# A ring of weight slots planned with other block times, and the second and third blocks' token rows fetched ahead of the routed experts' weights

## The reference

```python
for i in range(DEPTH):
    shift, scale, gate = adaln(cond, w_mod[i], b_mod[i])       # six vectors of 1024 per layer and condition
    x = x + g1 * mixer_i(modulate(x, norm_mix[i], sh1, sc1))
    x = x + g2 * moe(modulate(x, norm_ffn[i], sh2, sc2), ...)

def moe(h, ...):
    gates = top2_of_best_group(sigmoid(h @ w_router))          # (tokens, 16), two are not zero
    a, u = h @ w_gate[e], h @ w_up[e]                          # 1024 -> 256, for every expert e
    return sum_e((silu(a) * u * gates[:, e]) @ w_down[e])      # 256 -> 1024
```

## Time and profile before

| | |
|---|---|
| runs of the kernel before | 1649.26 us median of 3 (1647.81 to 1649.79) |
| profiled execution | 1657.81 us; span of its instructions 1656.0 us |
| TensorE busy | 1454.0 us, 88% of the span, granted clock 0.947 |
| VectorE, ScalarE, GpSimd busy | 556.2, 371.9 and 226.7 us |
| DMA | 417.21 MB, 252 GB/s over the span |

### The profile page before, as it was taken

One profiled execution on the slowest core, in us unless ns is written; L12 is line 12 of the kernel. 1 busy time (PEld: TensorE's weight loads), 2 busy tenths in 40 slices (PEclk: granted clock), 3 DMA queues, 4 the chain that ended last, 5 costly groups with the idle time before them and its releaser, 6 DMA issues.

```text
span 1656.0 us, 26585 instructions
## 1 busy us (share of the span) xinstructions
PE 1454.0 (88%) x10752; PEld 862.8 (52%) x10752; DVE 556.2 (34%) x1362; ACT 371.9 (22%) x985; POOL 226.7 (14%) x304
## 2 busy tenths in 40 slices
PE   3999998988997997997989999989869999969974
PEld 1876774323775774332564557743227766843221
DVE  1237343212456424211522442432105266242115
ACT  1106321110214521111211442211102045211110
POOL 0100122101121022111100001221011000221111
PEclk9999999998998998999899999999989999979997
DMA  9996148999788138899858403489997871247981
GB/s 328 320 320 196 77 173 292 384 413 349 262 304 233 78 134 280 305 421 349 296 197 246 120 1 153 173 298 387 399 345 258 280 270 55 98 164 302 422 338 56
DMA packets 122788, 417.21 MB, mean 252 GB/s; under 512 B 13659, under 2 KB 55614, under 8 KB 98086
## 3 DMA queue, kind: packets, MB, share of 16 engines
q1 hardware_dynamic: 95414, 345.08, 56.2%
q0 software_dynamic: 20304, 66.47, 12.2%
q10 hardware_dynamic: 6944, 3.91, 0.8%
HBM read 389.21 MB, written 28.76 MB: 252 GB/s over the span
## 4 chain that ended last, share of the span: by engine, by line
PE 70%; DVE 9%; DMA 8%; issue 6%; ACT 3%; POOL 1%; ACTq 1%; SPq 0%; another core or an unknown queue 0%; DVEq 0%; POOLq 0%
PE bank L1825 61%; DMA ring<-in_moe_w_gate 4%; PE bank L1995 3%; DMA hT<-h_rows,id_of 2%; PE bank L2159 2%; ACT pp L1147 2%; DMA ring<-in_moe_w_down 2%; ACTq L670 1%; PE bank L1882 1%; POOL small L804 1%; DVE xn L1294 1%; PE bank L2043 1%; DVE gbc L1291 1%; DVE xn L1304 1%; DVE hT L1281 0%
## 5 line engine op out<-in xcount | busy, mean ns | idle before, releaser
L1825 PE MATMUL bank<-ring,pp 128*32 128x512 f32 x2272 | 365.5, 634 | 40.6 <-DMA ring<-in_moe_w_down 27.9
L1825 PE MATMUL bank<-ring,hT 128*128 128x256 f32 (+3 forms) x998 | 234.9, 394 | 4.3 <-DVE kT L1590 2.6
L1825 PEld LDWEIGHTS bank<-ring,hT 128*128 128x128 f32 x998 | 182.5, 192 | 53.4 <-issue 27.9
L1825 PE MATMUL bank<-work,pp 128*32 128x512 f32 x816 | 183.9, 612 | 12.1 <-issue 9.2
L1825 PEld LDWEIGHTS bank<-ring,pp 128*32 128x32 f32 x2272 | 95.4, 116 | 167.1 <-issue 165.6
L1825 PE MATMUL bank<-ring,xn 128*128 128x256 f32 x768 | 168.2, 380 | 0.0
L1825 PEld LDWEIGHTS bank<-ring,xn 128*128 128x128 f32 x768 | 145.0, 190 | 19.4
L1825 PE MATMUL bank<-V,pp 128*32 128x512 f32 x512 | 131.0, 637 | 14.5 <-issue 11.6
L1715 DVE TENSOR_TENSOR pp<-bank,pp 128x256 f32<-128x256 f32 x40 | 17.0, 425 | 345.2 <-ACT pp L1224 345.2
L1147 ACT ACTIVATE pp<-bank,neg_max 128x384 f32<-128x384 f32 x192 | 96.6, 524 | 13.0 <-DVE neg_max L1606 10.1
L1825 PEld LDWEIGHTS bank<-work,pp 128*32 128x32 f32 x816 | 48.5, 112 | 94.5 <-issue 93.9
(11 more groups left out here) (275 smaller groups left out, 1800.1 us busy)
## 6 DMA issues: line engine op xcount, KB each, us to landing
ring<-in_w_mod SPq DMA_DIRECT2D x76, 1024.0 KB, 7.3
ring<-in_moe_w_gate SPq DMA_DIRECT2D x40, 1024.0 KB, 16.4
ring<-in_moe_w_up SPq DMA_DIRECT2D x40, 1024.0 KB
ring<-in_moe_w_down SPq DMA_DIRECT2D x37, 1024.0 KB, 14.5
work<-in_moe_w_down SPq DMA_DIRECT2D x16, 1024.0 KB, 7.9
y_slots<-kT POOLq DMA_DIRECT2D x32, 512.0 KB, 9.1
gbc<-in_w_mod SPq DMA_DIRECT2D x14, 1024.0 KB, 9.7
work<-in_moe_w_gate SPq DMA_DIRECT2D x12, 1024.0 KB
```

The source lines that it names most:

```text
L1825: return pe.matmul(out, lhsT, rhs, start=start, stop=stop)
```

## The change

The planner's block time goes from 11.8 to 12.05 us, the down tiles' first use from 11.0 to 18.3 us and their last from 18.5 to 22.8 us after their blocks' starts, and the stage starts 2 us later in the plan. d(12) to d(15) may now also stand in slots that only gate/up tiles used. mod(L+1,0,0) and mod(L+1,0,1) may use only slots 2 and 3, so that slots 0 and 1 can take an expert's pair early; the other six may use 4 to 7 and slot 13, which then waits for the mixer's last gate multiplication. DVE does `near_rows` ahead of `hold`, and `near_ids` ahead of its copy of block 0's rows. PE does `slot_ids` between the two halves of `gather_rows`. POOL issues two of the six writes to `ids`, then the rows of blocks 1 and 2, then tells SP (`near_issued`), then the other four writes. SP waits for both `held_ready` and `near_issued` before g(4).

```diff
@@ -193,13 +193,13 @@
         at = run_mods(mods["route"][:4], now + 52.0)
         run_mods(mods["route"][4:], at + 3.0)
         mark["held", L] = now + 68.0
-        now += 73.0
+        now += 75.0
         for e in range(E):
             for part in ("moe_g", "moe_u"):
-                begin[part, L, e], end[part, L, e] = now + 11.8 * first_block(e), now + 11.8 * last_block(e) + 7.5
-            begin["moe_d", L, e] = now + 11.8 * first_block(e) + 11.0
-            end["moe_d", L, e] = now + 11.8 * last_block(e) + 18.5
-        now += 11.8 * BLOCKS + 20.0
+                begin[part, L, e], end[part, L, e] = now + 12.05 * first_block(e), now + 12.05 * last_block(e) + 7.4
+            begin["moe_d", L, e] = now + 12.05 * first_block(e) + 18.3
+            end["moe_d", L, e] = now + 12.05 * last_block(e) + 22.8
+        now += 12.05 * BLOCKS + 19.0
         mark["summed", L] = now
     return begin, end, mark
 
@@ -219,10 +219,13 @@
         pairs = ((0, 1), (2, 3), (8, 9), (10, 11)) + (((4, 5),) if key[2] >= FIXED else ())
         return [pair if name == "moe_g" else pair[1:] for pair in pairs]
     if name == "moe_d":
-        return [(slot,) for slot in (6, 7, 12) + ((13,) if last_block(key[2]) < 7 else ())]
-    if name == "wo" or phase == "route" and key[2] == 1:
+        late = (13,) if last_block(key[2]) < 7 else tuple(range(6)) + (8, 9, 10, 11) if key[2] >= E - FIXED else ()
+        return [(slot,) for slot in (6, 7, 12) + late]
+    if name == "wo":
         return [(slot,) for slot in (4, 5, 6, 7)]
-    if name == "ukv" or phase == "route":
+    if phase == "route":
+        return [(2,), (3,)] if key[2:] in ((0, 0), (0, 1)) else [(slot,) for slot in (4, 5, 6, 7, 13)]
+    if name == "ukv":
         return [(slot,) for slot in (0, 1, 2, 3)]
     if name == "mod" and key[2] < 2:
         return [(slot,) for slot in range(R)]
@@ -237,6 +240,8 @@
         if slot in (10, 11):
             return mark["turned" if KINDS[L] < 2 else "heads", L]
         return mark[late[slot], L] if slot in late else 0.0
+    if part == "route":
+        return mark["mixed_in", L] if slot == 13 else 0.0
     return mark["summed", L - 1] if part == "main" and slot in (9, 13, 14) and L > 0 else 0.0
 
 
@@ -489,8 +494,8 @@
         rows_ready, wk_ready, over_ready, h_out, xT_full, xT_a, xT_v, ids_zeroed, ids_out, held_ready = (sem(s) for s in
             ("rows_ready", "wk_ready", "over_ready", "h_out", "xT_full", "xT_a", "xT_v",
              "ids_zeroed", "ids_out", "held_ready"))
-        near_ready, ids_full, ids_ready, ids_in, ov_t_in = (sem(s) for s in
-            ("near_ready", "ids_full", "ids_ready", "ids_in", "ov_t_in"))
+        near_ready, near_issued, ids_full, ids_ready, ids_in, ov_t_in = (sem(s) for s in
+            ("near_ready", "near_issued", "ids_full", "ids_ready", "ids_in", "ov_t_in"))
         g_in, y_out = [sem("g_in0"), sem("g_in1")], [sem("y_out0"), sem("y_out1")]
         (ov_idx_ready, ov_g_in, ov_xT_full, ov_xT_ready, ov_w_in, ov_au_full, ov_sil,
          ov_act, ov_acT_full, ov_acT_ready, ov_y_full, ov_y, ov_y_out) = (sem(s) for s in
@@ -706,10 +711,10 @@
                         sp.wait_ge(comb_used, 3 * L - 1)
                     elif slot == 14:
                         sp.wait_ge(x_moe_v, 3 * L)
+                elif slot == 13 and part != "main":
+                    sp.wait_ge(wo_mul, 12 * (L + 1))
                 elif part == "moe":
-                    if slot == 13:
-                        sp.wait_ge(wo_mul, 12 * (L + 1))
-                    elif slot in (10, 11) and KINDS[L] < 2:
+                    if slot in (10, 11) and KINDS[L] < 2:
                         wait_evacuated(sp, *[("qT", L, p) for p in range(8)], *[("kT", L, g) for g in range(G)])
                         sp.wait_ge(states, 32 * (L + 1))
                     elif slot >= R:
@@ -748,6 +753,7 @@
                     return
                 if (L, FIXED) not in held_at and e >= FIXED:
                     sp.wait_ge(held_ready, L + 1)
+                    sp.wait_ge(near_issued, L + 1)
                     held_at[L, FIXED] = None
                 if held_at.get((L, e)) is None:
                     at = e - FIXED
@@ -909,10 +915,13 @@
                 pool.wait_ge(rows_ready, L + 1)
                 if L == 0:
                     pool.wait_ge(ids_zeroed, 16)
-                for b in range(NB):
+
+                def ids_by_slot(b):
                     for k in range(2):
                         nc.gpsimd.indirect_dma_start(ids, rows_at(row_of[:, k, b:b + 1]), own_id[:, b:b + 1], None,
                                                      bounds_check=last_slot, oob_is_err=False).then_inc(ids_out, 16)
+
+                ids_by_slot(0)
                 pool.wait_ge(h_out, 48 * (L + 1))
                 pool.wait_ge(ids_ready, L + 1)
 
@@ -943,6 +952,9 @@
 
                 block_in(1)
                 block_in(2)
+                pool.sem_inc(near_issued, 1)
+                ids_by_slot(1)
+                ids_by_slot(2)
                 later_ids()
                 if L > 0:
                     pool.wait_ge(comb_full, 6 * L)
@@ -1688,8 +1700,8 @@
                 evacuate(*[("hrow", L, 2, half) for half in range(2)])
                 places(L)
                 slot_rows(L, picks)
+                near_rows(L)
                 hold(L)
-                near_rows(L)
                 pick_weights(L, picks)
                 overflow(L)
 
@@ -1707,8 +1719,8 @@
                     dve.wait_ge(ys_free, n + 1)
                     V_.tensor_copy(ys[:, blk % 2, 512:1024], bank[5][:, :]).then_inc(y_v, 1)
 
+                near_ids(L)
                 turned_rows(BLOCKS * L, 0)
-                near_ids(L)
                 for blk in range(BLOCKS):
                     n, slot = BLOCKS * L + blk, blk % 2
                     dve.wait_ge(sil_full, n + 1)
@@ -2232,6 +2244,8 @@
                     pe.wait_ge(xT_v, n + 1)
                     wait_evacuated(pe, *[("hrow", L, b, half) for b in range(NB) for half in range(2)])
                     for k in range(KC):
+                        if k == KC // 2:
+                            slot_ids()
                         for b in range(NB):
                             ins = mm(bank[6 + k // 4][:, k % 4 * P:(k % 4 + 1) * P], xn[:, b, k * P:(k + 1) * P],
                                      first_of[:, b, :], b == 0, b == NB - 1)
@@ -2284,7 +2298,6 @@
                     ins.then_inc(ids_full, 1)
 
                 gather_rows(BLOCKS * L)
-                slot_ids()
                 for blk in range(BLOCKS):
                     n, slot = BLOCKS * L + blk, blk % 2
                     block_gate_up(blk)
```

## The result

The changed kernel takes 1602.9 us (median of 4 runs, 1597.0 to 1608.5), the kernel before in the same comparison 1649.5 us: a ratio of 0.971, 95% interval 0.966 to 0.976. The prediction was 1601 us with a range of 1582 to 1630. A second comparison on the chip gave 0.973 (0.969 to 0.976). The profiled execution took 1606.3 us, with a span of 1604.5 us, 51.5 us less than before.

What follows compares the result with a forecast made beforehand. TensorE, busy 88% of the span, was taken as the bound, with late expert tiles setting the stage's end. Terms -51 + 1 + 1 = -49 us on 1657.8 gave 1609, in proportion 1601 us; range 1582 to 1630.

Steps and rivals of the forecast that it cites:

- The planner's list: Experts' stage: new tile order and slots let d(15) land earlier, gaining 10, 12, 18 and 11 us per layer, 51 us.
- The signs I named: Expected trace: no 15 us SP stand, d(15) issued over 10 us before last down, 405 GB/s over some 90 us.
- The anchor of the stream: Experts' stage: tile transfers counted from near_issued, with d(15) landing 127 us after it, 7 us of that for gaps.
- the slower rival: g(4) starts 8.6 us later per layer and the delay reaches the last down: 1669 us at 350 GB/s; chance 0.06.
- Near rows and numbers: Block 1's wait for gathered rows, 13.7 us in three layers, goes; none of it counted as gain, only as cover.
- The new wait: TensorE waits 2.6 to 3.9 us for the eighth modulation tile in layers 1 and 2; charged 1 us in all.
- The sum: All terms together: -51 + 1 + 1 = -49 us on the profiled 1657.8 us, in proportion 1601 us.
- slot_ids: Between the halves of block 0's rows: some 1.2 us, hidden in layers 0 to 2, about 1 us in layer 3.
- A gap that stays: Rival: pauses in the experts' tile stream remain or open elsewhere, giving 1636 us, or 1620 with half; chance 0.17.
- The late third gather: Rival: four later table writes delay block 3's rows, costing 5 us in three layers: 1616 us; chance 0.06.
- More: Rival: no gap and free table writes give 11 us more per layer, about 1577 us; chance 0.06.
- The ceiling of 358 GB/s: Rival: HBM loads can't pass 358 GB/s, so each layer ends about 2 us later: about 1659 us; chance 0.02.

Runs made afterwards that it cites:

- old modulation slots: The changed kernel with the eight modulation tiles back in the slots they had before the change: 1590.7 us, ratio 0.963; again 1601.0 us, 0.968.
- the front alone: Kernel before, old planner, with only near rows' numbers first, two gathers ahead of four table writes, and near_issued ahead of the first routed tile: 1653.3 us, 1.001.
- the modulation tile first: The changed kernel with the eighth modulation tile moved ahead of g(3), u(3) in SP's order, slots unchanged: 1594.2 us, ratio 0.966.
- both edits on the kernel before: Kernel before with the new block times and the new slots of the last four down tiles, modulation tiles and front as before: 1615.0 us, 0.976.
- the down slots alone: Kernel before with only the last four down tiles also allowed in slots that only gate/up tiles used: 1650.7 us, ratio 0.996.

## Why the prediction was right

The time was right to 2 us and the mechanism of the main term was right. That it came out so close is luck: the main term was too small by some 20 us, and the loss by the new wait too small by nearly as much.

- **The planner's list.** Predicted -51 us, by `near_issued` 10.8 us after the start of block 0's rows and d(15) landing 127 us behind it: 551 us over four layers from these rows to the last down. Measured 530.4, which is 72.2 less than before: g(4) leaves 7.1 to 9.0 us after the rows' start, and d(15) lands 123.1 to 124.9 us after g(4). Of the 72.2 us the stretch from block 2 to the last down has 59.5. The signs I named are all there: no 15 us stand of SP, d(15) out 20 us ahead of the last down, 414 GB/s for 80 us, short waits for tiles before block 7's down and block 9's gate/up (2.41 and 1.11 us). What I did not see is that it takes two edits. Block times order the gate/up pairs ahead of the downs, slots let the last downs go; one without the other moves the wait to the other end of the queue.
- **The anchor of the stream.** The step "d(15) lands 2.3 + 114 + 4 + 7 = 127 us after `near_issued`" has the right size for a wrong reason. The stream starts at the end of block 2's gate/up, which lies 31 to 32 us after g(4) in this kernel anyway. The run without the wait for `near_issued` tells the two apart: g(4) 7.1 us earlier, d(15) as late as before. The 8.6 us by which g(4) would be late, on which the slower rival rested, therefore cost nothing.
- **Near rows and numbers.** The step that failed is "I count none of it, since the down tiles set the end and these microseconds turn into waiting before block 9". The gather's wait went, as predicted, but it lies ahead of block 2 and so on the path. What that is worth depends on the rest. With the old modulation slots it is 12 us in the first column (169.0 to 156.9) and 14 us by medians. With the change's own slots it is 4 to 7 us by the ratios, inside the intervals, and 3.3 us in the first column (160.9 to 157.6): most of the 12.7 us there come with the planner. Alone it is worth nothing, as the run of the front alone shows. So for the change itself the step was wrong by little.
- **The new wait.** The charge of 1 us was mis-sized: the eighth modulation tile takes 6.30, 6.23 and 6.88 us of waiting, not 1.4 and 2.6 to 3.9. It lies on the path by the same anchor. In layer 0 the tile was issued at 249.0 behind g(3), u(3) and landed at 260.7, 11.6 us later, where I had 2.3 + 3 x 2.6 = 10.1. I had also counted it as covered by the gather's wait, which was itself no cover. After the wait the tile's records take 1.93 us where they take 1.07 without it. Moving the tile ahead brought 20.7 us back in the third column.
- **The sum.** -72.2 from the rows' start to the last down and +20.7 in all the rest (19.4 of it this wait), against my -51 and +2. The errors, 21.2 and 18.7 us, cancel to 2.5 us.
- **slot_ids.** 1.2 us predicted, 1.40 measured (266.33). It is not hidden in layer 0, where the rows' second half starts behind it.
- **The rivals.** A gap that stays: there is one, up to block 2 (282 GB/s), but from there none. The late third gather hardly came in the change (block 3's gather goes out at 291.2 in layer 0; its rows cost 0.2 and 0.6 us in layers 1 and 2). It came, with 7.6 to 9.7 us in all, in every run that has four table writes behind the gathers and no long wait for a modulation tile: the front alone, the modulation tile first, the old modulation slots. With the long wait it stays below 1 us a run. That the wait gives the table its time is my reading of this pattern; no run tests it. The rival "More" was priced wrong: by the prediction's own numbers TensorE is ready 128.1 us after the rows' start, which is 88 us of gain and some 1562 us, not 1577. The ceiling of 358 GB/s: the trace disagrees with that rule of the Trainium skill (page "DMA: Bandwidth & Descriptors", section "Where 436 GB/s comes from") less than I had put it. The 414 GB/s from 301 to 381 hold six stores of 0.52 MB, 39 GB/s, so loads alone ran at about 375 GB/s. That is still above the rule's figure, and the change gained.

What stays open: why the old modulation slots cost 10 to 15 us between block 2 and the last down (388.4 to 389.3 in the second column against 372.8 to 379.1). Late rows of block 3 are part of it where the front is new (8.5 and 7.9 us), but the run of both edits on the kernel before has none and shows 388.6. There TensorE's waits between the marks are 26.1 us against 15.4 in the change; they stand ahead of block 9's gate/up (2.8 to 4.3 us) and, in three layers, of the last down (3.2 to 4.5 us). Why the old slots make these tiles later I have not followed. Open too is whether these slots or the tile moved first are faster than the change by more than the spread of runs. No run has all three columns at their best; 154.6, 372.8 and 1053.4 would together make a span of some 1581 us, an estimate that takes the columns as independent.

## What to carry to other kernels

Before summing the work of a stream of transfers, find the tile that waits for a compute step and behind which the queue never runs empty. Here what delayed that step delayed the end, and the tiles that left ahead of it had 7 us to spare. Ask also what the compute engine's own work needs from that step on: here it was only 3 to 4 us per layer less. A strictly ordered list has a wait at each end of the queue, and mending its order or its slots alone only moves the wait: try them together before calling either useless. When a wait goes, look at what had stood behind it as "cover", for it is no cover any more.

## What the runs showed of the hardware

- A wait of 3 us costs TensorE about 5. The windows of block 7's gate/up in the run with the down slots alone, behind 3.10 us of waiting, and of block 8's gate/up in the change, with none:

```profile
355.70:364.50 8.80, 8.78 (x65) 2.91 (x66) 0.00 (x0) 0.00 (x0) 0.00 (x0) 0.81 1.01 421
```

```profile
368.40:375.50 7.10, 7.10 (x66) 2.07 (x66) 0.59 (x1) 0.54 (x2) 0.55 (x1) 1.00 1.02 421
```

The same 64 records take 8.8 us at a mean granted clock of 0.81 and 7.1 at 1.00. Part of the first stretch runs at 1.2 GHz instead of 2.4: from 358 to 360 of that run the granted clock is 0.52, from 360 to 362 it is 1.00. So the list of waits understates what a stretch of them costs.

- With a full queue a tile of 1.05 MB takes 19.2 us from issue to landing and one alone 4.9. With four more indirect writes of 128 numbers each ahead of it, a gather's rows came 2.6 to 3.4 us later in layers 0 to 2 (12.3 to 13.1 against 9.6 to 10.1 us from issue to TensorE's turn), with other tiles in flight in both runs.
